# HGRN's 32-token attention blocks on column groups and diagonal tiles, and dt's contraction tiles accumulated in place

## The chip, the cores and the metric

The kernel runs on one core of a Trainium2 chip. The metric is the device time of one execution in microseconds; shown are the median and the spread of three timed runs. Beside them there is a profile of one execution, taken by the hardware profiler, with the start and the duration of each instruction on each engine: TensorE (PE; its weight loads are listed as PEld), VectorE (DVE), ScalarE (ACT), GpSimd (POOL) and SyncE's DMA queue (SPq).

## The reference, cut to what matters

Two transformer blocks run one after the other on 256 tokens of width 1024, all in float32. The first mixes with an SSD and an RWKV branch; its input projection also makes `dt`, eight columns, one for each SSD head. The second mixes with an HGRN2 branch (4 heads of width 128) and an attention branch (MoBA), and goes on with cross-attention and an MLP. The parts that the change touches:

```
dt = softplus((xn @ w_in)[:, dt columns] + dt_bias)          # first block, 8 columns

# second block, HGRN2, C = 32 tokens a chunk, n = 8 chunks, 4 heads
b      = cumsum(log f) within a chunk
q_t    = q * exp(b);   k_t = k * exp(-b);   k_end = k * exp(b_last - b)
A      = where(causal, q_t k_t^T, 0)          # 32 x 32 for each chunk and head
o      = A v + q_t state                      # inside the chunk + from the chunks before
state  = decay * state + k_end^T v            # from chunk to chunk
o      = rms_norm(o) * gain * silu(gate)
```

## The kernel before

One program is written out by hand for each engine; the order on an engine is the order of the code, and engines wait for one another on semaphores (`mark` counts a step, `at` names the count to wait for). Nothing is scheduled by a planner. All 256 tokens stay in SBUF. Wide projections are split into two float16 halves by ScalarE and VectorE (lines 537 and 569) and multiplied in three float16 products (line 623); the small products of the mixers stay in float32. One float32 matmul stands in the trace as two records, each with its weight load.

**dt, first block.** Behind the tiles of the low-rank columns, TensorE makes dt's projection: eight contraction tiles `k` of 128 rows, each a matmul with 32 weight columns (the eight dt columns are the last of them) and 256 streamed tokens. Tile `k` goes to column group `k % 4` of the array (its output stands on PSUM partitions 32·(k % 4) and on) and to half `k // 4` of bank 5, so eight separate partial products lie there (line 958). VectorE scales them all by the norm's rate into `dt_parts`, 128x512 (line 1042). One tile of the r columns later, `pe_dt_fold` adds them up by two float32 matmuls with a selecting matrix (line 905), and ScalarE adds the bias (line 1127). The fold waits for the constants, which the POOL queue loads while w_in is still landing. Around it TensorE works on w_in's tiles (line 623).

**HGRN, second block.** `pe_project2` sets TensorE's order. The 256 tokens are cut into two groups `c` of 128, each with four 32-token chunks. `pe_hgrn` makes, for each `c` and head `j`, the product of all 128 keys with all 128 queries (`KF`, `HQ`; line 2739) into bank 4 + c, four heads side by side, 512 columns. `dve_hgrn` multiplies by the mask `chunk32` (line 2792), 128x128, which keeps the causal half of the four 32x32 blocks on the diagonal and sets all else to 0; the result is `AM[c]`. TensorE meanwhile turns `k_end` to token-major (line 2745) and works on a tile of the MoBA keys' projection (line 623), a small rotary product on four column groups (line 2859) and another tile of line 623. Then come the state products of single chunks (line 2756), the MoBA values (line 2540), and `pe_hgrn_out(c)`: `AM[c]` times the values `VI` into bank 6 + c (line 2767), and on top of it, for each chunk, the queries times the state before (line 2773), on column groups. VectorE carries the state from chunk to chunk (line 2805). Behind the HGRN stretch come the gate's projection, the MoBA attention, the turning of the output (line 2785) and the output projection (line 739), for which VectorE and ScalarE have to make halves first.

Small tiles stand elsewhere in the same kernel too. Line 1900, in RWKV's block solve of the first block, runs float32 matmuls with 32x32 weights and 16 streamed columns on the four diagonal tiles of the array, 16 for each of the two head groups, all of a group into one bank. Line 2000, RWKV's state update, has 64 weight columns on two column groups and streams 64. Line 1663 is the first TensorE work of RWKV's preparation, behind ScalarE's line 1708.

Of the kernel before, what the change touches and what calls it, by code (L numbers as in the profile page):

```python
# [17 lines left out]
ALU = mybir.AluOpType  # L18
# [5 lines left out]
P = 128  # L24
T = 256
D = 1024
KT = D // P
C = 128
# [25 lines left out]
W_SCALE = 64.0  # L54
# [17 lines left out]
for _name, _tiles in PARAM_TILES:  # L72
# [6 lines left out]
BASE = 32  # L79
# [2 lines left out]
    ("incl", P), ("strict", P), ("neg_incl", P),  # L82
    ("ident32", BASE), ("pair32", BASE), ("levels", BASE // 2 * len(LEVELS)),
    ("blocks64", 2 * BASE),
    ("chunk32", P), ("causal", T), ("swap", P), ("cos", T), ("sin", T),
    ("reset128", T), ("reset32", T),
]
CONST_AT = {}
# [7 lines left out]
def constant_table():  # L96

    out = np.zeros((P, CONST_COLS), np.float32)

    def put(name, value):  # L100
        at, w = CONST_AT[name]
        out[:value.shape[0], at:at + w] = value

    r, c = np.arange(P)[:, None], np.arange(P)[None, :]
    put("ident", np.eye(P))
    put("ones", np.ones((P, P)))
    put("head_ones", (r // RW_HD == c // RW_HD) * 1.0)
    put("incl", (r <= c) * 1.0)
    put("strict", (r < c) * 1.0)
    put("neg_incl", (r <= c) * -1.0)  # L110
    r32, c32 = r % BASE, np.arange(BASE)[None, :]
    put("ident32", (r32 == c32) * 1.0)
    put("pair32", ((c32 == r32 + 1) & (c32 % 2 == 1)) * -1.0)
    put("blocks64", (np.arange(2 * BASE)[None, :] // BASE == r // BASE % 2) * -1.0)
    levels = []
    for m in LEVELS:

        mask = ((r32 // (2 * m) == c32 // (2 * m)) & (r32 % (2 * m) >= m) & (c32 % (2 * m) < m)) * 1.0
        levels.append(mask.reshape(P, BASE // (2 * m), 2, m)[:, :, 0, :].reshape(P, BASE // 2))
    put("levels", np.concatenate(levels, axis=1))  # L120
    put("chunk32", ((r <= c) & (r // HG_CHUNK == c // HG_CHUNK)) * 1.0)
    q, k = np.arange(P)[:, None], np.arange(T)[None, :]
    put("causal", np.where(k - P <= q, 0.0, -3e38))
    half = ROT // 2
    swap = np.zeros((P, P))
    for i in range(half):
        swap[i + half, i] = 1.0
        swap[i, i + half] = 1.0
    put("swap", swap)
    inv = np.float32(ROPE_THETA) ** (-np.arange(half, dtype=np.float32) * np.float32(2.0) / np.float32(ROT))  # L130
    ang = np.arange(T, dtype=np.float32)[:, None] * inv[None, :].astype(np.float32)
    cos, sin = np.cos(ang).T, np.sin(ang).T
    put("cos", np.concatenate([cos, cos]))
    put("sin", np.concatenate([-sin, sin] * MB_HEADS))
    t = np.arange(T)[None, :].repeat(P, 0)
    put("reset128", (t % C != 0) * 1.0)
    put("reset32", (t % HG_CHUNK != 0) * 1.0)
    return out
# [170 lines left out]
def build(nc, w, out, known):  # L309

    with ExitStack() as ctx:
# [38 lines left out]
        def const(name):  # L350
            a, n = CONST_AT[name]
            return consts[:, a:a + n]
# [60 lines left out]
        zs = view(SOLVE + 4128, 4, T)  # L413
        BTOKS = view(SOLVE + 5152, 2, SSD_STATE)
        dtT, aT, dtmp = view(SOLVE + 7168, T), view(SOLVE + 5664, T), view(SOLVE + 5920, T)
        dt_parts = view(SOLVE + 5664, 2, T)
        dtok = view(SOLVE + 6176, NC_, 8)
        atok = view(SOLVE + 6192, NC_, 8)
        cstok = view(SOLVE + 6208, NC_, 8)
# [480 lines left out]
        def pe_dt_fold(pe):  # L900

            pe.wait_ge(*at("dt raw"))
            pe.wait_ge(*at("constants landed"))
            for i in range(2):
                mm = nc.tensor.matmul(banks[6][0:SSD_HEADS, 0:T], const("ident32")[:, BASE - SSD_HEADS:BASE],
                                      dt_parts[:, i, :], start=(i == 0), stop=(i == 1))
            mm.then_inc(*mark("proj1_dt", "dt folded"))

        def pe_project1(pe):
            pe_project1_first(pe)  # L910
            for i, (kind, j) in enumerate(TILE_OF):
# [42 lines left out]
                if kind == "lora" and j == 1:  # L954

                    for k in range(KT):
                        q = BASE * (k % 4)
                        mm = nc.tensor.matmul(halves(5)[q:q + BASE, k // 4, :], slot("w_in", "lora")[:, k, 232:264],
                                              hg[:, k, :], start=True, stop=True, tile_position=(0, q))
                    mm.then_inc(*mark("proj1_dt", "proj1 dt"))  # L960
                    chunk_used("w_in", "lora", 0, ("proj1 dt",))
                elif j == dict(PROJ)[kind] - 1:
                    if ("w_in", kind, 0) in SPLIT_NO:
                        split_used(("w_in", kind, 0), ("proj1", b))
                    else:
                        chunk_used("w_in", kind, 0, ("proj1", b))
# [64 lines left out]
        def dve_project1_rwkv(dve):  # L1031
            lora_low(dve)
            norm_reciprocal(dve, "pre_mix")
            dve.wait_ge(*so_far("norm_rstd"))
            for b in range(7):
                dve.wait_ge(*at("proj1", b))
                if b == 0:
                    dve.wait_ge(*at("pads"))
                evacuate1(raw[:, 2 * b:2 * b + 2, 1:T + 1], b).then_inc(*mark("proj1_scaled", "proj1 out", b))
                if b == 2:  # L1040
                    dve.wait_ge(*at("proj1 dt"))
                    nc.vector.scalar_tensor_tensor(dt_parts, halves(5), 1.0 / W_SCALE, over(rstd[:, :], 2), ALU.mult,
                                                   ALU.mult).then_inc(*mark("dt_raw", "dt raw"))
                if b in (0, 2):
                    split_low(dve, b // 2, range(4))
                if b == 3:
                    split_low(dve, 2, range(4))
                if b == 4:
                    dve_shift(dve, range(3))
                    bc_low(dve, (0, 1))  # L1050
                if b == 5:
                    bc_low(dve, (2,))
            bc_low(dve, (3,))
            dve_shift(dve, range(3, 7))
# [1460 lines left out]
        FR, BCS, EB, EMB, HQ, KF = (view(1024 * i, 4, T) for i in range(6))  # L2515
        KETOK, VI = view(1024, NC_, HG_D), view(7168, NC_, HG_D)
        GH = view(8192, 4, T)
        AM = [view(512 * i, 4, C) for i in range(2)]
        NS = T // HG_CHUNK
        SV = [view(a, 4 * C) for a in (3072, 3584, 5120, 5632, 13312, 15872)] + [ssum[:, :]]  # L2520
        ON = view(3072, NC_, HG_D)
# [210 lines left out]
        def pe_hgrn(pe):  # L2732
# [3 lines left out]
            pe.wait_ge(*at("k~"))  # L2736
            for c in range(NC_):
                for j in range(4):
                    mm = nc.tensor.matmul(quarters(4 + c)[:, j, :], KF[:, j, c * C:(c + 1) * C],
                                          HQ[:, j, c * C:(c + 1) * C], start=True, stop=True)  # L2740
                mm.then_inc(*mark("hgrn_pe", "A bank", c))
            pe.wait_ge(*at("k end"))
            for c in range(NC_):
# [18 lines left out]
        def pe_hgrn_out(pe, c):  # L2762
# [1 line left out]
            pe.wait_ge(*at("A", c))  # L2764
            pe.wait_ge(*at("k end token-major", c))
            for j in range(4):
                nc.tensor.matmul(quarters(6 + c)[:, j, :], AM[c][:, j, :], VI[:, c, j * C:(j + 1) * C],
                                 start=(j == 0), stop=False, skip_group_check=True)
            pe.wait_ge(*at("hgrn state", 4 * c + 2))
            for j in range(4):  # L2770
                for n in range(max(1, 4 * c), 4 * c + 4):
# [17 lines left out]
        def dve_hgrn(dve):  # L2789
            for c in range(NC_):  # L2790
                dve.wait_ge(*at("A bank", c))
                nc.vector.tensor_tensor(AM[c], quarters(4 + c), over(const("chunk32"), 4), ALU.mult).then_inc(
                    *mark("hgrn_vector", "A", c))

        def dve_hgrn_state(dve, n):
            dve.wait_ge(*at("hgrn state bank", n))
# [786 lines left out]
```

## Time and profile before

| | |
|---|---|
| timed runs | 742.17, 743.42 and 743.67 us; median 743.42 |
| the profiled execution | span 741.7 us from its first to its last instruction, the one time that its page gives |
| TensorE busy | 730.6 us, 98% |
| VectorE, ScalarE, GpSimd busy | 576.3, 435.5 and 47.1 us |
| chain that ended last | TensorE 78%, VectorE 12%, ScalarE 4%, DMA 4% |
| A products, line 2739 | 16 records in 1.79 us |
| A times V, line 2767 | 2 x 8 records, 0.89 us each |
| dt's fold, line 905 | 4 records |

The chain of work that ended last is followed back from the last instruction, at each step to what released it. A group in it holds the time from the end of what came before it to its own end. Time saved in a group that is not in the chain shortens nothing by itself. Matmuls are pipelined: the duration of one record covers its way through the array, so the rate of a group is read from the starts of groups or from the chain, not from the duration of one.

### The profile page before, as it was taken

The numbers are of one execution on the slowest core, as the hardware profiler recorded it, in microseconds if no ns is written. First come the engines' busy times: TensorE is split into PE (matmuls) and PEld (weight loads), VectorE is DVE, ScalarE is ACT, GpSimd is POOL, SyncE is SP. The second block draws the span as 40 slices with busy tenths as digits, with TensorE's granted clock in tenths as the row PEclk, the third lists the DMA queues.
The fourth block names the chain that finished last, engine by engine and source line by source line (L and its number), as shares of the span: only waits on it lengthen the run. The fifth ranks groups of instructions, "written<-read, shape, count | busy, mean of one in ns | idle before, by whom it ended". The sixth has DMA issues, their size and how long they took to land.

```text
span 741.7 us, 16496 instructions
## 1 busy us (share of the span) xinstructions
PE 730.6 (98%) x7072; PEld 597.3 (81%) x7072; DVE 576.3 (78%) x908; ACT 435.5 (59%) x679; POOL 47.1 (6%) x81
## 2 busy tenths in 40 slices
PE   9999999999999999999999999999999999999997
PEld 6888877889778888888877686898888888865553
DVE  5899976777889999998678887899786666762444
ACT  5699872523656766666656573487584655653342
POOL 0000133040020000000002000003003000000000
PEclk9999999999999999999999999999999999999999
DMA  9990303512574566557690743339326165566001
GB/s 316 395 401 5 114 17 139 206 38 81 179 275 146 196 228 224 177 175 253 240 353 1 266 189 114 115 114 340 116 89 252 48 241 174 221 227 219 37 0 58
DMA packets 67146, 129.43 MB, mean 174 GB/s; under 512 B 3969, under 2 KB 28033, under 8 KB 66817
## 3 DMA queue, kind: packets, MB, share of 16 engines
q1 hardware_dynamic: 66032, 126.07, 47.2%
q0 software_dynamic: 320, 1.61, 0.6%
q8 instruction: 56, 0.92, 0.5%
q10 hardware_dynamic: 720, 0.70, 0.3%
q14 instruction: 18, 0.14, 0.1%
HBM read 127.32 MB, written 1.05 MB: 173 GB/s over the span
## 4 chain that ended last, share of the span: by engine, by line
PE 78%; DVE 12%; ACT 4%; DMA 4%; issue 1%; SPq 0%; DVEq 0%; ACTq 0%
PE bank L623 35%; PE bank L3218 11%; PE bank L739 11%; DVE arena L569 3%; PE bank L2540 3%; DMA ring<-in_w_in_dram 2%; PE bank L1551 2%; PE bank L874 1%; PE bank L1570 1%; PE bank L1832 1%; DMA ring<-in_ffn_w_up_dram 1%; PE bank L893 1%; DVE arena L1076 1%; PE bank L1885 1%; PE bank L2012 1%
## 5 line engine op out<-in xcount | busy, mean ns | idle before, releaser
L623 PE MATMUL bank<-hg,arena 128*128 128x256 f16 x2496 | 275.4, 273 | 1.5 <-DVE arena L556 1.1
L623 PEld LDWEIGHTS bank<-hg,arena 128*128 128x128 f16 x2496 | 243.6, 98 | 32.6 <-issue 2.6
L569 DVE SCALAR_TENSOR_TENSOR arena<-ring,arena 128x1024 f16<-128x1024 f32 x150 | 175.5, 1227 | 52.7 <-ACT arena L537 52.7
L537 ACT ACTIVATE arena<-ring 128x1024 f16<-128x1024 f32 x150 | 146.6, 1044 | 83.8 <-PE bank L3218 37.6
L3218 PE MATMUL bank<-arena 128*128 128x512 f16 (+1 forms) x480 | 83.6, 336 | 0.0
L3218 PEld LDWEIGHTS bank<-arena 128*128 128x128 f16 x480 | 47.0, 98 | 36.1
L739 PE MATMUL bank<-arena 128*128 128x256 f16 x528 | 57.8, 273 | 0.0
L739 PEld LDWEIGHTS bank<-arena 128*128 128x128 f16 x528 | 51.7, 98 | 6.0
L556 DVE SCALAR_TENSOR_TENSOR arena<-ring,arena 128x2048 f16<-128x2048 f32 x22 | 50.4, 2292 | 0.7
L739 PE MATMUL bank<-mix,arena 128*128 128x256 f16 x384 | 42.2, 273 | 0.0
L549 ACT ACTIVATE arena<-ring 128x2048 f16<-128x2048 f32 x22 | 41.7, 1895 | 0.0
L739 PEld LDWEIGHTS bank<-mix,arena 128*128 128x128 f16 x384 | 37.6, 98 | 4.3
L2491 ACT ACTIVATE arena<-arena,params 128x256 f32<-128x256 f32 x44 | 20.0, 500 | 31.8 <-DVE arena L2437 31.8
L623 PE MATMUL bank<-xv,arena 128*128 128x256 f16 x336 | 37.4, 273 | 0.2 <-issue 0.2
L2448 DVE SCALAR_TENSOR_TENSOR arena<-arena,params 128x256 f32<-128x256 f32 x88 | 36.7, 479 | 0.7 <-ACT arena L2491 0.7
L623 PEld LDWEIGHTS bank<-xv,arena 128*128 128x128 f16 x336 | 32.5, 98 | 5.4 <-DVE arena L569 0.8
L638 ACT ACTIVATE hg<-h,params 128x256 f16<-128x256 f32 x32 | 15.9, 498 | 26.4 <-DVE h L799 13.4
L658 POOL TENSOR_TENSOR ssum<-sqs 128x256 f32<-128x256 f32 x4 | 2.9, 728 | 351.8 <-ACT sqs L642 351.8
L3172 DVE SCALAR_TENSOR_TENSOR arena<-bank,rstd 128x512 f32<-128x512 f32 x16 | 11.0, 690 | 16.3 <-PE bank L623 16.3
L648 DVE SCALAR_TENSOR_TENSOR hg<-h,params,hg 128x256 f16<-128x256 f32 x32 | 20.4, 658 | 3.9 <-ACT hg L638 3.9
L1570 PE MATMUL bank<-arena,xk 128*128 128x512 f16 x96 | 21.4, 379 | 0.0
L2540 PE MATMUL bank<-arena,hg 128*128 128x512 f16 x96 | 21.2, 379 | 0.0
(425 smaller groups left out, 992.5 us busy)
## 6 DMA issues: line engine op xcount, KB each, us to landing
ring<-in_w_in_dram SPq DMA_DIRECT2D x12, 2048.0 KB, 9.7
ring<-in_ffn_w_up_dram SPq DMA_DIRECT2D x22, 1024.0 KB, 7.8
ring<-in_w_ff_dram SPq DMA_DIRECT2D x8, 2048.0 KB, 8.9
ring<-in_w_ff_dram SPq DMA_DIRECT2D x16, 1024.0 KB, 6.6
ring<-in_ffn_w_down_dram SPq DMA_DIRECT2D x11, 1024.0 KB, 6.6
ring<-in_w_out_dram SPq DMA_DIRECT2D x8, 1024.0 KB, 7.7
ring<-in_w_xk_dram SPq DMA_DIRECT2D x2, 2048.0 KB, 11.8
ring<-in_w_xv_dram SPq DMA_DIRECT2D x2, 2048.0 KB, 10.3
```

Source lines behind the costliest of these rows:

```text
L537: nc.scalar.activation(quarter(halves_of(chunk)[0], chunk, q), quarter(slot(*chunk), chunk, q), ACT.Copy, scale=W_SCALE).then_inc(*mark("w ...
L549: nc.scalar.activation(pair_of(halves_of(chunk)[0], chunk, q), pair_of(slot(*chunk), chunk, q), ACT.Copy, scale=W_SCALE).then_inc(*mark("w ...
L556: nc.vector.scalar_tensor_tensor(pair_of(halves_of(chunk)[1], chunk, q), pair_of(slot(*chunk), chunk, q), W_SCALE, pair_of(halves_of(chunk ...
L569: nc.vector.scalar_tensor_tensor(quarter(halves_of(chunk)[1], chunk, q), quarter(slot(*chunk), chunk, q), W_SCALE, quarter(halves_of(chunk ...
L623: mm = nc.tensor.matmul(out_, weight[a][:, k, cols], src[:, k, b, :], start=(first and i == 0), stop=(last and i == 2), skip_group_check=True)
L648: nc.vector.scalar_tensor_tensor(hg16[:, m, 1, :], h[:, m, :], par(gain, m), hg16[:, m, 0, :], ALU.mult, ALU.subtract).then_inc(*mark("nor ...
L739: mm = nc.tensor.matmul(out_, weight, moving[:, k, b, :], start=(first and n == 0), stop=(last and n == 2), skip_group_check=True)
L1570: mm = nc.tensor.matmul(banks[2 + c][:, :], mem16[:, k, x, c * C:(c + 1) * C], w_[a][:, k, :], start=(k == 0 and i == 0), stop=(k == KT - ...
L2448: nc.vector.scalar_tensor_tensor(uacc[r][:, i, :], uraw[r][:, i, tap:tap + T], par("ffn_conv_w", 2 * FFT * tap + tile0 + i), uacc[r][:, i, :],
L2491: nc.scalar.activation(uacc[r][:, i, :], uraw[r][:, i, 2:T + 2], ACT.Copy, scale=par("ffn_conv_w", 2 * 2 * FFT + 2 * p + FFT * (b % 2) + i ...
L2540: mm = nc.tensor.matmul(banks[bank][:, :], hg16[:, k, b, c * C:(c + 1) * C], w_[a][:, k, :], start=(k == 0 and n == 0), stop=(k == KT - 1 ...
L3218: mm = nc.tensor.matmul(last_bank(c, half, cols)[:, cols], hid2[:, k, x, c * C:(c + 1) * C], weight[a][:, k % 4, 512 * half + cols.start:5 ...
```

## The change

A products: instead of one 128x128 product for each head and token group, four products of 32 keys with 32 queries, one for each chunk. Chunk `b` goes to column group `b` and stands on PSUM partitions 32·b to 32·b + 31, head `j` in columns 32·j and on, so that a token group's blocks fill 128 columns of a bank instead of 512. The mask shrinks to 32 columns, the same causal triangle on each 32 partitions, and `AM[c]` to 128x128. A times V uses the block of chunk `b` as a 32x32 weight on the diagonal tile (row group `b`, column group `b`), against that chunk's 32 rows of values, 128 columns wide: 16 matmuls for 4. The matmuls of dt keep their number and their column groups, but tiles `k` and `k + 4` now accumulate in the same 256 columns, so VectorE scales 128x256 and the fold is one matmul. The table of constants loses 96 columns, and its load goes from 1056 KB to 1008 KB.

```
@@ constants
-    ("chunk32", P), ("causal", T), ("swap", P), ("cos", T), ("sin", T),
+    ("chunk32", BASE), ("causal", T), ("swap", P), ("cos", T), ("sin", T),
...
-    put("chunk32", ((r <= c) & (r // HG_CHUNK == c // HG_CHUNK)) * 1.0)
+    put("chunk32", (r % HG_CHUNK <= np.arange(HG_CHUNK)[None, :]) * 1.0)
@@ dt
-            for i in range(2):
-                mm = nc.tensor.matmul(banks[6][0:SSD_HEADS, 0:T], const("ident32")[:, BASE - SSD_HEADS:BASE],
-                                      dt_parts[:, i, :], start=(i == 0), stop=(i == 1))
-            mm.then_inc(*mark("proj1_dt", "dt folded"))
+            nc.tensor.matmul(banks[6][0:SSD_HEADS, 0:T], const("ident32")[:, BASE - SSD_HEADS:BASE], dt_parts,
+                             start=True, stop=True).then_inc(*mark("proj1_dt", "dt folded"))
...
-                        mm = nc.tensor.matmul(halves(5)[q:q + BASE, k // 4, :], slot("w_in", "lora")[:, k, 232:264],
-                                              hg[:, k, :], start=True, stop=True, tile_position=(0, q))
+                        mm = nc.tensor.matmul(banks[5][q:q + BASE, 0:T], slot("w_in", "lora")[:, k, 232:264],
+                                              hg[:, k, :], start=(k < 4), stop=(k >= 4), tile_position=(0, q),
+                                              skip_group_check=True)
...
-                    nc.vector.scalar_tensor_tensor(dt_parts, halves(5), 1.0 / W_SCALE, over(rstd[:, :], 2), ALU.mult,
+                    nc.vector.scalar_tensor_tensor(dt_parts, banks[5][:, 0:T], 1.0 / W_SCALE, rstd[:, :], ALU.mult,
@@ HGRN
-                    mm = nc.tensor.matmul(quarters(4 + c)[:, j, :], KF[:, j, c * C:(c + 1) * C],
-                                          HQ[:, j, c * C:(c + 1) * C], start=True, stop=True)
+                    for b in range(4):
+                        r, t = HG_CHUNK * b, c * C + HG_CHUNK * b
+                        mm = nc.tensor.matmul(banks[4 + c][r:r + HG_CHUNK, HG_CHUNK * j:HG_CHUNK * (j + 1)],
+                                              KF[:, j, t:t + HG_CHUNK], HQ[:, j, t:t + HG_CHUNK], start=True,
+                                              stop=True, tile_position=(0, r))
...
-                nc.tensor.matmul(quarters(6 + c)[:, j, :], AM[c][:, j, :], VI[:, c, j * C:(j + 1) * C],
-                                 start=(j == 0), stop=False, skip_group_check=True)
+                for b in range(4):
+                    q = slice(HG_CHUNK * b, HG_CHUNK * b + HG_CHUNK)
+                    nc.tensor.matmul(quarters(6 + c)[q, j, :], AM[c][q, j, :], VI[q, c, j * C:(j + 1) * C],
+                                     start=(j == 0), stop=False, tile_position=(HG_CHUNK * b, HG_CHUNK * b),
+                                     skip_group_check=True)
...
-                nc.vector.tensor_tensor(AM[c], quarters(4 + c), over(const("chunk32"), 4), ALU.mult).then_inc(
-                    *mark("hgrn_vector", "A", c))
+                nc.vector.tensor_tensor(AM[c], banks[4 + c][:, 0:P].rearrange("p (j n) -> p j n", j=4),
+                                        over(const("chunk32"), 4), ALU.mult).then_inc(*mark("hgrn_vector", "A", c))
```

No instruction changes its place on its engine. Here is what stands on TensorE in a row around the A products, before (the first row is the column form of the norm's rate, line 623 is a projection, 2745 turns k_end, 2859 is the rotary product; the shape is the output's, and a float32 matmul is one row here and two records in the trace):

```order
L697 MATMUL bank<-consts,rstd 128x1 x2
L623 MATMUL bank<-hg,arena 128x256 x144
L2739 MATMUL bank<-arena 128x128 x8
L2745 MATMUL bank<-consts,arena 128x128 x8
L623 MATMUL bank<-hg,arena 128x256 x24
L2859 MATMUL bank<-arena,consts 32x256 x4
```

And in the changed kernel, whose line numbers have moved a little:

```order
L697 MATMUL bank<-consts,rstd 128x1 x2
L623 MATMUL bank<-hg,arena 128x256 x144
L2740 MATMUL bank<-arena 32x32 x32
L2747 MATMUL bank<-consts,arena 128x128 x8
L623 MATMUL bank<-hg,arena 128x256 x24
L2864 MATMUL bank<-arena,consts 32x256 x4
```

Eight full products have become 32 small ones in the same place, between two groups on the full array. On TensorE around A times V of the first token group, before (2756 are state products, 2540 the MoBA values, 2773 queries times states, 2889 and 2890 MoBA scores):

```order
L2756 MATMUL bank<-arena 128x128 x8
L2540 MATMUL bank<-arena,hg 128x512 x24
L2767 MATMUL bank<-arena 128x128 x4
L2773 MATMUL bank<-arena 32x128 x12
L2756 MATMUL bank<-arena 128x128 x8
L2889 MATMUL bank<-arena 128x128
L2890 MATMUL bank<-arena 128x256
```

And now:

```order
L2758 MATMUL bank<-arena 128x128 x8
L2539 MATMUL bank<-arena,hg 128x512 x24
L2771 MATMUL bank<-arena 32x128 x16
L2778 MATMUL bank<-arena 32x128 x12
L2758 MATMUL bank<-arena 128x128 x8
L2894 MATMUL bank<-arena 128x128
L2895 MATMUL bank<-arena 128x256
```

Four full matmuls have become 16 on 32x32 tiles; the second token group changes in the same way.

## Rows read from the trace of the kernel before

**Rows 1.** The page: busy us (share) xinstructions of each engine; the chain's shares by engine.

```profile
PE 730.6 (98%) x7072; PEld 597.3 (81%) x7072; DVE 576.3 (78%) x908; ACT 435.5 (59%) x679; POOL 47.1 (6%) x81
...
PE 78%; DVE 12%; ACT 4%; DMA 4%; issue 1%; SPq 0%; DVEq 0%; ACTq 0%
```

**Rows 2.** The chain of work that ended last, HGRN stretch: start us, us, what.

```profile
443.59 1.79 PE bank L2739 x16
...
446.25 2.62 PE bank L623 x24
...
449.43 2.73 PE bank L623 x24
...
465.48 0.89 PE bank L2767 x8
...
475.36 0.89 PE bank L2767 x8
476.25 1.01 PE bank L2773 x32
```

**Rows 3.** The timeline, 436 to 470 us: start us, us, engine line op out<-in xcount [idle before].

```profile
443.43 1.95 PE L2739 MATMUL bank<-arena 128*128 128x128 f32 x16
...
445.38 1.28 DVE L2792 TENSOR_TENSOR arena<-bank,consts 128x512 f32<-128x512 f32 x2
...
449.50 0.43 DVE L2874 TENSOR_TENSOR bank<-bank,consts 128x256 f32<-128x256 f32 x1 [2.84 <-PE bank L2859]
```

**Rows 4.** The timeline of TensorE, 119 to 127 us.

```profile
120.10 0.73 PE L1900 MATMUL bank<-arena 32*32 32x16 f32 x64
120.76 1.48 PE L1551 MATMUL bank<-xk,sqs 128*128 128x256 f16 x12
```

**Rows 5.** The timeline of TensorE, 137 to 140 us.

```profile
137.71 1.15 PE L2000 MATMUL bank<-arena 128*64 128x64 f32 x32
138.69 1.48 PE L2012 MATMUL bank<-arena 128*64 128x128 f32 x24
```

**Rows 6.** The chain of work that ended last, first 68 us.

```profile
18.60 18.16 DMA ring<-in_w_in_dram
...
66.33 0.95 ACT arena L1708
...
67.33 0.76 PE bank L1663 x5
```

**Rows 7.** Who waited for whom, VectorE and ScalarE, 426 to 512 us: us, times, longest.

```profile
DVE arena L2805 <- PE bank L2756: 3.6, 2, 2.0
...
ACT mix L2965 <- PE bank L2912: 1.4, 2, 0.7
```

**Rows 8.** Who waited for whom, TensorE, whole span: us, times, longest.

```profile
PE bank L1663 <- ACT arena L1708: 0.6, 1, 0.6
```

**Rows 9.** The timeline, 27.9 to 36.2 us.

```profile
28.16 0.68 DVE L1042 SCALAR_TENSOR_TENSOR arena<-bank,rstd 128x512 f32<-128x512 f32 x1
...
31.39 4.63 DVE L569 SCALAR_TENSOR_TENSOR arena<-ring,arena 128x1024 f16<-128x1024 f32 x4 [2.55 <-ACT arena L537]
...
33.08 1.03 PE L905 MATMUL bank<-arena,consts 128*8 128x256 f32 x4
...
34.04 2.36 PE L623 MATMUL bank<-xv,arena 128*128 128x256 f16 x20
```

**Rows 10.** DMA issues, 10 to 60 us (KB, us to landing); then a stretch, DMA share, GB/s.

```profile
consts<-in_constants_dram POOLq DMA_DIRECT2D x1, 1056.0 KB, 9.1
...
22.00:26.00 4.00, 4.00 (x45) 2.93 (x44) 3.79 (x5) 4.00 (x6) 1.36 (x3) 1.00 1.05 404
```

**Rows 11.** Stretches: us, busy us (xcount) by engine, granted clock, DMA share, GB/s.

```profile
110.00:115.00 5.00, 5.00 (x58) 3.73 (x55) 0.63 (x3) 0.26 (x1) 0.00 (x0) 0.85 0.01 3
115.00:120.00 5.00, 5.00 (x113) 3.89 (x112) 3.90 (x11) 1.65 (x2) 0.00 (x0) 0.80 0.02 3
...
440.00:446.00 6.00, 6.00 (x57) 5.65 (x56) 6.00 (x8) 2.49 (x4) 0.00 (x0) 1.00 0.31 128
```

More of the change, by code:

```diff
@@ L415, in build @@
         dtT, aT, dtmp = view(SOLVE + 7168, T), view(SOLVE + 5664, T), view(SOLVE + 5920, T)
-        dt_parts = view(SOLVE + 5664, 2, T)
+        dt_parts = view(SOLVE + 5664, T)
         dtok = view(SOLVE + 6176, NC_, 8)
@@ L2517, in build @@
         GH = view(8192, 4, T)
-        AM = [view(512 * i, 4, C) for i in range(2)]
+        AM = [view(512 * i, 4, HG_CHUNK) for i in range(2)]
         NS = T // HG_CHUNK
```

## The prediction

> **What bounds the kernel now.** I read the page's busy times first, then the chain of work that ended last, then the two stretches that the change touches. TensorE is busy 98% of the span and holds 78% of that chain [rows 1], so a microsecond of TensorE counts only where the chain runs through TensorE. In the HGRN stretch it does: from 443 to 490 us the chain goes from one TensorE group straight to the next, and the three groups that the change rewrites stand in it by name [rows 2]: the A products (line 2739) and the two A times V products (line 2767). In the dt stretch it does not: from 18.60 to 36.76 us the chain is the landing of w_in, after that VectorE and ScalarE, and TensorE comes back only at 67.33 us, where it had waited 0.6 us for ScalarE's line 1708 [rows 6, 8].
>
> **The A products.** Before, 8 matmuls of 128x128 make 16 records (one f32 matmul is two) [rows 3], and they hold 1.79 us of the chain [rows 2], 0.112 us a record. Three quarters of what they make is masked away. After, 32 matmuls of 32x32 make 64 records, four of them side by side on the four column groups, each streaming 32 columns instead of 128. The nearest rows are those of line 1900: 64 f32 records, also four side by side, 32 columns loaded and 16 streamed, start at 120.10 us, and the next group starts at 120.76: 0.66 us, with the way out into a full-array group in it [rows 4]. The way in costs something too. 24 matmuls of line 623 behind another full-array group hold 2.62 us, the same 24 behind the 32-row rotary matmuls 2.73 [rows 2]: a change of tile shape costs 0.11. So the new A costs 0.66 + 0.11 = 0.77 us, and the term is 0.77 - 1.79 = **-1.02 us**. The trace has no f32 tile of 128 rows by 32 columns that streams as few columns as it loads. The row that bounds it on the dear side is line 2000, which loads 64 columns of 128 rows and streams 64: 32 records in sixteen pairs from 137.71 to 138.69 us, 0.98 us [rows 5]. If a round of four new tiles took as long as such a pair, A would cost 0.98 + 0.11 = 1.09, a gain of 0.70. I take 1.02, since line 1900 has the same number of records, rounds and loaded columns; what it lacks is 96 rows of weights and 16 streamed columns. Nothing in the rows is quicker than line 1900, so the gain's upper end is 1.1.
>
> **A times V.** Before, 4 matmuls (8 records) for each of the two 128-token chunks hold 0.89 us [rows 2]. After, 16 matmuls (32 records) on four diagonal 32x32 tiles, each still streaming 128 columns. Four side by side therefore last as long as one full matmul: the stream isn't shortened, only rows and columns of the array are left out. The row like it is line 2773 of the second chunk: 32 f32 records, four side by side, 128 streamed columns, 1.01 us with its own change of shape [rows 2]. So each product goes from 0.89 to 1.01, **+0.12**, twice: **+0.24 us**. The change of shape behind it (into line 2773) was there before. This is what the smaller A tile costs, for the compact block can only be used on diagonal tiles.
>
> **VectorE's masking.** Two products of 128x512 take 1.28 us and become 128x128. Behind them VectorE waits 2.84 us for TensorE's rotary matmul [rows 3], so this is worth nothing here. It only uncovers a longer wait; the cover would have to shrink by 2.84 us before it counted.
>
> **Does the HGRN gain reach the end?** Later work on VectorE and ScalarE in this stretch waits for TensorE and not the other way: VectorE's state update waits 3.6 us in all for line 2756, ScalarE's copies of the MoBA output 1.4 us for line 2912 [rows 7]. These waits move with TensorE; where a stage's release is not moved at all, 0.7 us (the longest wait of line 2965) of the 0.78 would still pass. I count the whole: -1.02 + 0.24 = **-0.78 us**.
>
> **dt.** The eight dt matmuls stay eight and of the same shape; only their start and stop flags and half of their addresses change: 0. VectorE's scaling of 128x512 (0.68 us) becomes 128x256, which saves at most half, 0.34; but the next VectorE group waits 2.55 us for ScalarE, which waits for w_in to land [rows 9]: 0. The fold's four records run from 33.08 to 34.04 us, 0.96 [rows 9]; two of them fall away, some 0.43 us of TensorE. TensorE then reaches the wait at 67.33 us that much sooner and waits 1.0 instead of 0.6 [rows 8]: 0. It would be worth 0.43 if the chain ran through TensorE there.
>
> **The constants.** The mask shrinks from 128 to 32 columns, so the load of 1056 KB becomes 1008 KB. It runs in the very stretch in which the chain is the landing of w_in, at 404 GB/s over all engines [rows 6, 10]. 48 KB at that rate is **-0.12 us**, at least 0 if the two don't share engines evenly.
>
> **Sum.** -0.78 - 0.12 = -0.90 us. The profiled execution has a span of 741.7 us, 1.7 below the median of 743.42; nothing in the change touches what lies around the span. 743.42 - 0.90 = **742.5 us**. With the bounds (A's gain 0.70 to 1.1, the constants 0 to 0.12, the fold 0 to 0.43) the sum lies between -0.46 and -1.41, 742.0 to 743.0, and the timed runs themselves spread from 742.17 to 743.67.
>
> **Rivals.** *Small records start one by one.* If the records, not the rounds of four, set the pace, with line 2000's 0.98 / 32 = 31 ns a record, 64 of them take 1.96 + 0.11 = 2.07 us, and A loses 0.28; the sum is 0.28 + 0.24 - 0.12 = +0.40, 743.8. Against it: line 1900's 64 records in 0.66 us are 10 ns each [rows 4]. The Trainium skill states such a floor ("TensorE: Matmul & The Clock Gate", section "Wait — 56ns, not 53.3ns?"): starts never closer than about 25 ns however few columns are streamed. By that rule A would take 1.6 + 0.11 = 1.71 us, the sum would be +0.04, and the trace's 10 ns contradict it for tiles that lie side by side. Chance 0.07.
>
> *Diagonal tiles that write one bank take turns: slower.* All four diagonal tiles of A times V write one PSUM bank from different rows of the array. If they ran one after the other, each of the 32 records would cost what a full record does, 0.89 / 8 = 0.111 us: 3.56 + 0.11 = 3.67 for 0.89, +2.78 twice; the sum is -1.02 + 5.56 - 0.12 = +4.4, 747.8. It turns the sign as soon as the two products together lose over 1.14 us. Against it: line 1900 also runs four diagonal tiles into one bank, and at 10 ns a record they overlap. But it streams only 16 columns, so a conflict would show less there. The Trainium skill says of row tiles that they can't use the same PSUM bank at the same time ("TensorEngine Tiling (Array Packing)", section "Gotcha 1: PSUM Pressure"); line 1900's 0.66 us [rows 4] speak against it. Chance 0.03.
>
> *The gain is taken back before 490 us*, by a VectorE or ScalarE chain that doesn't move with TensorE: only the constants are left, 743.3. Chance 0.07; rows 7 speak against it.
>
> *The clock.* The granted clock is 1.00 in every stretch around the change, but between 110 and 120 us it is 0.85 and then 0.80 [rows 11], behind small matmuls: lost clock of 0.75 + 1.00 = 1.75 us at most. A similar fall to 1.2 GHz at the new small matmuls would give 742.5 + 1.75 = 744.3 at most (0.04), and the fall at 110 us gone, through a shift of the work, 740.8 at least (0.04).
>
> *The fold counts*: 742.1 (0.05). *A at its dear bound*: 742.8 (0.08).
>
> **How the numbers follow.** That leaves 0.62 for the forecast. A measurement of this kernel can tell about 0.2%, 1.5 us, from no change; the forecast is 0.9 below, so it would mostly read as the same. Given the spread of the runs I let a quarter of its 0.62 fall below 741.9, half of the fold's case and all of the lifted clock: 0.22 faster. Slower holds the turn-taking tiles and a little of the clock's fall: 0.04. The rest, 0.74, is the same. The range takes the bounds of the sum, the first and third rivals and most of the spread of the runs: 741.4 to 743.9.
>
> **What would show it.** In the changed kernel the chain's A group should hold 64 records in some 0.7 to 0.8 us where 1.79 stood, with four starts close together and then a short pause; each A times V group 32 records in 1.0 us; VectorE's two masks some 0.6 us together and the wait behind them longer; the fold two records; the wait before line 1663 longer than 0.6 us; w_in's landing at 36.76 some 0.1 us earlier. It is wrong if the A records stand 20 ns or more apart, if the A times V group goes over 1.5 us, if TensorE waits between 445 and 490 us where it didn't, or if the clock falls in that stretch.

## The result and the profile after

The changed kernel takes 744.99 us (median of 20 runs, 743.15 to 747.44) and the kernel before, beside it, 743.64 (20 runs, 742.17 to 744.48). The ratio is 1.0024, with a 95% interval of 1.0015 to 1.0032: slower by some 1.8 us, where 0.9 us less was forecast. (The ratio is not the quotient of the two medians, which lie 1.35 us apart; prices in us are taken from the ratios, here and below, unless the text says otherwise.) The profiled execution has a span of 742.6 us (741.7 before) and an own time of 744.4.

The page of the changed kernel (busy us, share of the span, instructions; then the shares of the chain of work that ended last), to be held against [rows 1]:

```profile
PE 729.5 (98%) x7166; PEld 595.6 (80%) x7166; DVE 575.4 (77%) x908; ACT 435.4 (59%) x679; POOL 47.0 (6%) x81
...
PE 78%; DVE 12%; ACT 5%; DMA 4%; issue 1%; SPq 0%; DVEq 0%; ACTq 0%
```

TensorE has 1.1 us less work and 94 records more (96 more in A and A times V, two less in the fold), and yet the span is longer. The sum of the busy times doesn't say where it went; the chain does. The chain of the changed kernel (start us, us, what; it counts 50 of A's 64 records, the timeline further down has them all):

```profile
26.05 17.24 DMA ring<-in_w_in_dram
...
194.33 9.16 DMA ring<-in_ffn_w_up_dram
...
445.08 0.69 PE bank L2740 x50
445.77 1.02 PE bank L2747 x8
...
466.02 1.01 PE bank L2771 x32
...
476.02 1.01 PE bank L2771 x32
...
490.84 0.60 ACT mix L2970
```

The HGRN groups behave as forecast against [rows 2]: A holds 0.69 us where 1.79 stood, each A times V product 1.01 where 0.89 stood. But the A products begin at 445.08 us and not at 443.59. The loss lies ahead of them, where nothing of HGRN has run yet: the landing of w_up, for one, holds 9.16 us of the chain. The same rows of the kernel before, with the end of its HGRN stretch:

```profile
193.50 8.50 DMA ring<-in_ffn_w_up_dram
...
490.07 0.60 ACT mix L2965
```

I then laid VectorE's instructions of the two traces beside each other, in the order of the program, and took the difference of their starts. The changed kernel is late by 1.5 us at 49 us, by 0.5 at 116 and 0.3 at 120, by 0.8 at 159, by 1.5 again at 206 and by 0.8 at 484. The step at 116 to 120 us belongs to TensorE's clock. The kernel before was granted 0.85 and 0.80 from 110 to 120 us in its profiled execution [rows 11]; the changed kernel, in the same two stretches (us, busy us and count by engine, granted clock, DMA share, GB/s):

```profile
110.00:115.00 5.00, 4.58 (x64) 4.42 (x65) 1.85 (x8) 1.32 (x3) 0.51 (x2) 1.00 0.01 3
115.00:120.00 5.00, 5.00 (x116) 3.64 (x114) 3.42 (x9) 1.65 (x2) 0.00 (x0) 1.00 0.01 3
```

So the two spans alone, 0.9 us apart, hide 1.2 us: that execution of the kernel before had lost it to the clock, this one had not. What is left is lateness of 1.5 us that arises before 50 us and of 0.7 around 204 us, in the two stretches in which the chain is the landing of weights, and half a microsecond at 155 us, among RWKV's small matmuls, where the DMA engines are all but idle. From 22 to 40 us (the same columns), first the kernel before, then the changed one:

```profile
22.00:40.00 18.00, 18.00 (x167) 14.72 (x166) 13.99 (x15) 13.09 (x19) 1.36 (x3) 1.00 1.05 395
```

```profile
22.00:40.00 18.00, 18.00 (x170) 14.92 (x167) 13.37 (x15) 12.63 (x18) 1.76 (x3) 1.00 1.04 378
```

The DMA engines are as busy (a share of 1.05 and 1.04) and move 378 GB/s where they moved 395. The forecast had no term for that. The change's one touch on any DMA is the table of constants, 96 columns of fp32 shorter.

### The profile page after: what moved, and what is told of

The parts are those of the page before. It is cut to its first block, busy times and chain, and to the rows that moved or that the text cites. A ratio compares the mean times of both kernels' runs of the same rounds, so it can differ in the third digit from the quotient of the medians.

```text
span 742.6 us, 16684 instructions
## 1 busy us (share of the span) xinstructions
PE 729.5 (98%) x7166; PEld 595.6 (80%) x7166; DVE 575.4 (77%) x908; ACT 435.4 (59%) x679; POOL 47.0 (6%) x81
## 3 DMA queue, kind: packets, MB, share of 16 engines
HBM read 127.27 MB, written 1.05 MB: 173 GB/s over the span
## 4 chain that ended last, share of the span: by engine, by line
PE 78%; DVE 12%; ACT 5%; DMA 4%; issue 1%; SPq 0%; DVEq 0%; ACTq 0%
PE bank L623 35%; PE bank L3223 11%; PE bank L739 11%; PE bank L2539 3%; DVE arena L569 3%; DMA ring<-in_w_in_dram 2%; PE bank L1550 2%; PE bank L874 1%; PE bank L1569 1%; DMA ring<-in_ffn_w_up_dram 1%; PE bank L1831 1%; PE bank L893 1%; PE bank L2011 1%; DVE arena L611 1%; PE bank L819 1%
```

## Experiments

Each edit is timed in five rounds against the kernel before on the same chip. The first four ran together, the next four, the next three, and the last one alone.

**Which part of the change it is.** Two causes were open: the landings, through the table, and the clock, through the new small matmuls, in executions that no profile shows. Three kernels carry one part each, and the fourth is the whole change again. HGRN alone has the change's hunks in HGRN, with the table of constants left as wide as before (its mask uses the first 32 of 128 columns):

```
-    put("chunk32", ((r <= c) & (r // HG_CHUNK == c // HG_CHUNK)) * 1.0)
+    put("chunk32", (r % HG_CHUNK <= np.arange(P)[None, :]) * 1.0)
...
+  ... over(const("chunk32")[:, 0:HG_CHUNK], 4), ALU.mult)
```

> The kernel before with the HGRN edits alone (A on column groups, A times V on diagonal tiles, the smaller mask product); the table of constants keeps its size, so the SBUF layout and the transfers are those of before; dt as before. Theory clock: the small tiles leave TensorE so little to do between 445 and 480 us that its clock is lowered to 1.2 GHz there in many executions; then this kernel has mean granted clocks down to 0.993 to 0.997 in its timed runs, a wide spread, and a median 0.5 to 2 us above before although the profile's HGRN groups are 0.78 us shorter. Theory layout: the loss comes from the smaller table of constants and the 384 bytes by which all of SBUF moves; then this kernel is 0.6 to 0.8 us faster than before, with the clocks of before.

Measured: 742.06 us against 743.32, ratio 0.9988 (0.9977 to 0.9999). The HGRN edits gain some 0.9 us, near the 0.78 of the sum. Its executions had mean granted clocks of 0.993 to 1.000, those of the kernel before that they are compared with 0.996 to 1.000, and it was the quicker one all the same: the small matmuls don't cost it the clock in its median.

dt alone has only the change's hunks in dt.

> The kernel before with the dt edits alone (accumulated in one half bank, scaled 128x256, one fold matmul). Theory clock and theory layout both: within 0.3 us of before, since the fold is off the chain. A third theory, that the shorter fold lets TensorE run into the stage behind it in another way: 0.5 us or more off, in either direction.

Measured: 743.55 against 743.32, ratio 1.0000 (0.9991 to 1.0009). No gain is seen, as forecast; but the interval is 0.7 us to either side, and the fold's 0.43 us could hide in it.

The table alone is the kernel before, with another table cut by the same 96 columns. The rotary swap table is used in its first 32 columns only, so no instruction changes but the load:

```
-    ("chunk32", P), ("causal", T), ("swap", P), ("cos", T), ("sin", T),
+    ("chunk32", P), ("causal", T), ("swap", BASE), ("cos", T), ("sin", T),
...
-    put("swap", swap)
+    put("swap", swap[:, 0:BASE])
```

> The kernel before with another table cut from 128 to 32 columns (the rotary swap matrix, of which only 32 columns are used), so that the load of constants and the place of everything in SBUF behind it are exactly those of the changed kernel, and the program is that of before. Theory layout: 1 to 2 us slower than before, the packets of w_in between 20 and 40 us some 5% longer (90 ns against 86) and w_in's landing that ends the first chain 1 us later. Theory clock: as before, or 0.1 us faster.

Measured: 745.41 against 743.32, ratio 1.0025 (1.0015 to 1.0035). A kernel that loads 48 KB less and does nothing else differently is slower by some 1.9 us. The window of 22 to 40 us in its trace:

```profile
22.00:40.00 18.00, 18.00 (x168) 14.72 (x166) 13.75 (x15) 12.44 (x17) 1.76 (x3) 1.00 1.04 379
```

and in the trace of HGRN alone:

```profile
22.00:40.00 18.00, 18.00 (x168) 14.72 (x166) 14.49 (x16) 13.59 (x19) 1.62 (x3) 1.00 1.05 397
```

379 GB/s with the shorter table, 397 with the table as it was: the slow landings come and go with the table, and neither with HGRN nor with dt.

> The changed kernel once more beside the kernel before on this chip. Both theories: 1.0 to 1.8 us slower than before. Theory clock: the slow executions are those with a low mean clock. If instead the difference came from the chip of the first comparison, it is 0.5 to 1 us faster here.

Measured: 743.91 against 743.32, ratio 1.0010 (1.0001 to 1.0019); 379 GB/s in the window. The whole change is again slower than before, by 0.7 us, which is less than in the first comparison and less than both theories expected; the two intervals overlap from 1.0015 to 1.0019 only. The parts add up to -0.12 + 0.00 + 0.25 = +0.13%.

**What about a shorter table makes landings slower.** The constants are the first tensor in SBUF, and params and the weight ring follow. Cutting 96 columns moves all that lies behind by 384 bytes in each partition. The ring, into which every weight lands, began at byte 11392 of a partition, counted from the start of the constants by the widths in the code, 128 over a multiple of 256; now it begins at 11008, a multiple of 256. If the address counts and not the load, unused columns ahead of the ring must give the time back, and take it away from the kernel before. Four kernels put them there:

```
         consts = sb("consts", CONST_COLS)
+        sb("pad", 96)
         params = sb("params", PARAM_COLS)
         ring = sb("ring", RING, SLOT)
```

The changed kernel with 96 columns has its ring at 11392 again.

> The changed kernel with an unused 96-column tile in SBUF behind the table of constants, so that all of SBUF behind it stands where it stood before, while the table and its load stay small (1008 KB). Theory address (the place of the weight ring in SBUF sets how fast the weights land): as the HGRN edits alone, 0.8 to 1.4 us faster than before, packets of w_in at 84 ns. Theory transfer (the smaller load, or what it moves in HBM, is what costs): 0.6 to 1.5 us slower than before, packets at 88 ns.

Measured: 741.95 against 742.86, ratio 0.9988 (0.9978 to 0.9999). 384 unused bytes in each partition turn the change from slower to faster.

The kernel before with 32 columns there has its ring at 11520, a multiple of 256, and its load of constants untouched.

> The kernel before with an unused 32-column tile behind the table of constants: its table and load stay at 1056 KB, but the ring and all behind it move up by 128 bytes, to the same remainder of 512 bytes (256) as in the changed kernel. Theory address: 1.5 to 2.5 us slower than before, packets of w_in at 87 to 88 ns. Theory transfer: as before, 84 ns.

Measured: 745.61 against 742.86, ratio 1.0031 (1.0016 to 1.0045): the loss without any part of the change.

The changed kernel with 64 columns (11264, a multiple of 512) asks whether a rounder address is better.

> The changed kernel with an unused 64-column tile there: the ring begins at a multiple of 512 bytes. Theory address: not the time of the changed kernel; if whole multiples suit the packets best, 1.0 to 2.5 us faster than before; if 128 bytes over a multiple was a lucky place, 0 to 2 us slower. Theory transfer: as the changed kernel, 0.6 to 1.5 us slower than before.

Measured: 744.58 against 742.86, ratio 1.0016 (1.0002 to 1.0029): it isn't.

The changed kernel with 32 columns (11136, again 128 over a multiple of 256, but not the place of the kernel before) asks whether it is that one place or the remainder.

> The changed kernel with an unused 32-column tile there: the ring begins 384 bytes over a multiple of 512. Theory address: packets differ from one of the other places; 128 and 384 may be alike (84 ns, 0.8 to 1.4 us faster than before) if it is the multiple of 256 that costs. Theory transfer: as the changed kernel.

Measured: 742.19 against 742.86, ratio 0.9987 (0.9977 to 0.9997): it is the remainder. The window of 22 to 40 us in the four traces, with 96 columns in the changed kernel, 32 in the kernel before, 64 and 32 in the changed kernel:

```profile
22.00:40.00 18.00, 18.00 (x170) 14.92 (x168) 14.19 (x15) 13.56 (x19) 1.70 (x3) 1.00 1.05 396
```

```profile
22.00:40.00 18.00, 18.00 (x167) 14.72 (x166) 13.02 (x14) 12.38 (x17) 1.76 (x3) 1.00 1.05 377
```

```profile
22.00:40.00 18.00, 18.00 (x169) 14.93 (x168) 13.12 (x15) 12.36 (x17) 1.76 (x3) 1.00 1.04 377
```

```profile
22.00:40.00 18.00, 18.00 (x170) 14.92 (x168) 14.05 (x15) 13.41 (x19) 1.54 (x3) 1.00 1.05 397
```

396 and 397 where the ring begins 128 over, 377 and 377 on a multiple of 256. The pair of the changed kernel with and without 96 columns is the cleanest, since both run the same instructions. The chain with the 96 columns (its lines are one further down):

```profile
25.68 15.95 DMA ring<-in_w_in_dram
...
192.10 8.56 DMA ring<-in_ffn_w_up_dram
...
442.26 0.69 PE bank L2741 x50
442.95 1.02 PE bank L2748 x8
...
463.20 1.00 PE bank L2772 x32
...
473.20 1.00 PE bank L2772 x32
...
488.02 0.60 ACT mix L2971
```

The landing of w_in holds 15.95 us where 17.24 stood, that of w_up 8.56 where 9.16 stood. VectorE without the columns is late by 0.9 us at 23 us, 1.6 at 49, 2.0 at 154 and 2.8 at 203, behind w_up, and stays so to the end (742.6 against 739.7 us of span). Not all of that is landings: 0.6 us of it arises between 150 and 159 us, where the chain without the columns has TensorE pause twice for 0.14 us inside line 1899 (0.55 + 0.14 + 0.37 us for a group that holds 0.72 with the columns) and no weight is waited for. The traces of the whole change again and of the 64 columns below, compared with the same one, are later by 0.3 us and by nothing there, so at least half of that step belongs to this one execution. Without it the spans give the price of the landings as 2.9 - 0.6 = 2.3 us, and the ratios of two such kernels timed together (1.0016 with 64 columns, 0.9988 with 96) as 0.28%, 2.1 us.

The DMA issues between 20 and 60 us (KB, us from issue to landing), without and with the 96 columns, show the load that was to bring the gain:

```profile
ring<-in_w_xk_dram SPq DMA_DIRECT2D x1, 2048.0 KB, 15.6
...
consts<-in_constants_dram POOLq DMA_DIRECT2D x1, 1008.0 KB, 9.2
```

```profile
ring<-in_w_xk_dram SPq DMA_DIRECT2D x1, 2048.0 KB, 14.7
consts<-in_constants_dram POOLq DMA_DIRECT2D x1, 1008.0 KB, 8.8
```

The smaller load itself took 9.2 us, not less than the 9.1 of before [rows 10], and 8.8 with the ring back in its place; that it was held up by the weights, which land more slowly on the same engines, is likely but not shown.

**The ring, or what lies behind it.** Columns ahead of the ring move everything behind it too. Two kernels separate them: the changed kernel with 32 columns ahead and 32 more behind the ring (ring 128 over; all behind it at the changed kernel's remainder), and one with 32 behind the ring alone (the other way round). Params, ahead of the ring, moves with it.

```
+        sb("pad", 32)
         params = sb("params", PARAM_COLS)
         ring = sb("ring", RING, SLOT)
+        sb("pad_behind", 32)
```

> The changed kernel with 32 unused columns ahead of the weight ring and 32 behind it: the ring begins 128 bytes over a multiple of 256, all that stands behind it (activations, arena) a whole multiple of 256, as in the changed kernel. Theory ring (only the place that the DMA writes counts): as the changed kernel with its padding, 0.8 to 1.4 us faster than before, packets at 84 ns. Theory rest (what the engines read and write while the weights land, the arena and the activations, is what must stand at 128): 0.6 to 1.5 us slower than before, packets at 88 ns.

Measured: 742.19 against 743.49, ratio 0.9988 (0.9979 to 0.9997).

> The changed kernel with 32 unused columns behind the weight ring alone: the ring stays at a whole multiple of 256 bytes, all behind it moves to 128 over one. Theory ring: as the changed kernel, 0.6 to 1.9 us slower than before, packets at 88 ns. Theory rest: 0.8 to 1.4 us faster than before, 84 ns.

Measured: 745.46 against 743.49, ratio 1.0025 (1.0013 to 1.0037). The place of the ring, with params that move with it, is all of it; what lies behind the ring doesn't count. The windows of the two:

```profile
22.00:40.00 18.00, 18.00 (x169) 14.92 (x168) 14.01 (x16) 13.13 (x18) 1.76 (x3) 1.00 1.04 393
```

```profile
22.00:40.00 18.00, 18.00 (x170) 14.93 (x168) 12.81 (x14) 11.45 (x16) 1.76 (x3) 1.00 1.05 377
```

**Other remainders.** With 16 columns the ring begins at 11072, 64 over a multiple of 256, and with 48 at 11200, 192 over.

> The changed kernel with 16 unused columns behind the table of constants: the ring begins 64 bytes over a multiple of 256. If only whole multiples of 256 are slow: packets at 84 ns and 0.8 to 1.4 us faster than before. If 128 is the one good place: packets above 84 ns and slower than before.

Measured: 745.51 against 743.49, ratio 1.0026 (1.0016 to 1.0037).

> The changed kernel with 48 unused columns behind the table of constants: the ring begins 192 bytes over a multiple of 256. If 128 over is the one good place among multiples of 64: packets slower than 84 ns, 0.6 to 2.2 us slower than before. If 192 is good too: 84 ns and 0.8 to 1.4 us faster than before.

Measured: 745.85 against 742.55, ratio 1.0040 (1.0026 to 1.0053): 3.0 us slower, more than the 2.2 that was expected at most. The windows of the two:

```profile
22.00:40.00 18.00, 18.00 (x170) 14.93 (x168) 12.85 (x15) 12.34 (x17) 1.76 (x3) 1.00 1.04 375
```

```profile
22.00:40.00 18.00, 18.00 (x169) 14.91 (x168) 13.19 (x15) 12.50 (x18) 1.76 (x3) 1.00 1.04 378
```

Of the four remainders, in steps of 64 bytes, 128 alone is good:

| ring begins, bytes over a multiple of 256 | kernels | GB/s, 22 to 40 us | packet of 2048 bytes, median, 40 to 55 us |
|---|---|---|---|
| 128 | before, HGRN alone, dt alone, 96 columns, 32 columns, ring alone | 393 to 397 | 84 ns |
| 0 | changed, table alone, before with 32, 64 columns, rest alone | 377 to 379 | 88 ns |
| 64 | 16 columns | 375 | 88 ns |
| 192 | 48 columns | 378 | 88 ns |

Finer steps than 64 bytes weren't tried, nor another tensor than the ring.

## Why the prediction was wrong, step by step

**The constants: the step that failed.** The prediction gave the shorter table -0.12 us, "at least 0 if the two don't share engines evenly". It priced the table as bytes of one load. Cut alone, the table costs +0.25%, 1.9 us (1.1 to 2.6 by the interval of its ratio), through a route that was not in the list: it is the first tensor in SBUF, so its width sets the address of the weight ring, and 384 bytes put every weight landing in a place where the same DMA engines, as busy as before, move 4 to 5% less (22 to 40 us). The bound "at least 0" had no row behind it; the diff alone tells that everything behind the table moves. The landing that was to end 0.1 us earlier than 36.76 us [rows 6] ends later. The changed kernel's chain takes another piece of w_in, but that of the table alone has one that begins 0.7 us later than the row of before:

```profile
19.26 18.82 DMA ring<-in_w_in_dram
```

It ends at 38.08 us, 1.3 us later, and took 18.82 us for 18.16.

**A products: right.** Forecast 0.66 + 0.11 us for 1.79. The timeline of the changed kernel (start us, us, engine line op, tile, shapes, records):

```profile
445.01 0.76 PE L2740 MATMUL bank<-arena 128*32 128x32 f32 x64
...
445.70 1.09 PE L2747 MATMUL bank<-consts,arena 128*128 128x128 f32 x8
...
446.87 0.48 DVE L2797 TENSOR_TENSOR arena<-bank,consts 128x128 f32<-128x128 f32 x2
...
450.05 0.43 DVE L2879 TENSOR_TENSOR bank<-bank,consts 128x256 f32<-128x256 f32 x1 [2.70 <-PE bank L2864]
```

From the first A record to the first transpose 0.69 us pass. The transposes behind now hold 1.02 us of the chain where they held 0.87 in the kernel before:

```profile
445.38 0.87 PE bank L2745 x8
```

The change of tile shape now lies there, and the two groups together go from 1.79 + 0.87 = 2.66 to 0.69 + 1.02 = 1.71: -0.95 for a forecast of -1.02. Line 1900 was the right row to price it by: 128 rows and 32 streamed columns cost no more than its 32 and 16.

**A times V: right.** 1.01 us for 0.89, twice, +0.24. The rows of the first product and of the group behind it:

```profile
465.95 1.08 PE L2771 MATMUL bank<-arena 32*32 32x128 f32 x32
...
466.96 1.07 PE L2778 MATMUL bank<-arena 128*32 128x128 f32 x24
```

32 records in 1.01 us on four diagonal tiles that write one bank: they run side by side.

**VectorE's masks: right.** 0.48 us for 1.28 [rows 3], worth nothing: VectorE waits 2.70 us behind them, 2.84 before. The wait was to grow and did not: the masks end 0.80 us sooner, but TensorE's products, and with them the rotary matmul, come 0.95 us sooner.

**Does the HGRN gain reach the end: right.** From the start of A to line 2965 (now 2970) 490.07 - 443.59 = 46.48 us pass before and 490.84 - 445.08 = 45.76 after, a gain of 0.72; the terms measured give -0.95 + 0.24 = -0.71. Alone, the HGRN edits gain 0.12% (0.01 to 0.23) at the end, and the three versions of the change with the ring 128 over a multiple of 256 gain as much.

**dt: right in its sizes; what it is worth is not settled.** VectorE's scaling takes 0.41 us for 0.68, the fold two records from 33.89 to 34.42 us, 0.53 for 0.96 [rows 9]. The changed kernel's timeline:

```profile
29.40 0.41 DVE L1041 SCALAR_TENSOR_TENSOR arena<-bank,rstd 128x256 f32<-128x256 f32 x1
...
33.89 0.60 PE L904 MATMUL bank<-arena,consts 128*8 128x256 f32 x2
34.42 3.34 PE L623 MATMUL bank<-xv,arena 128*128 128x256 f16 x29
```

The wait ahead of line 1663 (now 1662) was to go from 0.6 to 1.0 us. It is 1.7:

```profile
PE bank L1662 <- ACT arena L1707: 1.7, 1, 1.7
```

but the late weights are in this number: with the ring back in its place the same wait is 0.4 us, so the forecast of 1.0 is not borne out. The wait that was to swallow dt's gain isn't a fixed reserve either. In the traces of HGRN alone and of dt alone it is not there at all: from 25 to 67 us their chain is TensorE's own work, and the fold stands in it, first as before, then as one matmul:

```profile
33.41 0.96 PE bank L905 x4
```

```profile
34.10 0.53 PE bank L904 x2
```

So, with the ring 128 over a multiple of 256, TensorE and the landings end this stretch within a microsecond of each other, and which of them ends last differs from one trace to the next. The forecast's 0 for the fold came from one execution in which the landings did. The time of dt alone doesn't tell 0 from 0.43 us.

**The rivals.** Small records one by one fell: 0.69 us for 64 records is 10.8 ns each, the way in with it, and not 31. The rule of the Trainium skill that was weighed there ("TensorE: Matmul & The Clock Gate", section "Wait — 56ns, not 53.3ns?"), starts never closer than about 25 ns, doesn't hold for these tiles side by side: in the trace the first starts come in fours 7 ns apart, a four every 32 ns. Diagonal tiles that take turns fell at 1.01 us against 3.67; the skill's rule on one PSUM bank ("TensorEngine Tiling (Array Packing)", section "Gotcha 1: PSUM Pressure") doesn't show in these products. The gain taken back before 490 us fell with the 45.76 us, A at its dear bound with the 0.69 us; the fold is open, as said. The fall of the clock at the new matmuls would have given about the time that came, 744.3, but by another cause. In the changed kernel's HGRN stretch it stays at full speed (2.4 GHz):

```profile
440.00:491.00 51.00, 50.99 (x559) 38.83 (x557) 42.33 (x98) 24.14 (x43) 0.00 (x0) 1.00 0.30 110
```

The clock does move single executions: of HGRN alone, five at a mean clock below 0.998 took 742.9 to 745.0 us, and seven at 0.998 or over 741.1 to 742.2. But both kernels have such executions, and the ring's price stands at an equal clock too: of the executions at 0.999 or over, those of the kernel before with 32 columns took 744.1 to 745.4 us, those of the kernel before beside it 742.0 to 743.5, and those of the changed kernel with 96 columns 741.1 to 742.3. The other half of that rival, the fall at 110 us gone, is what the two profiled executions show, and in them it covered part of the loss. The HGRN and dt edits don't take it away: the changed kernel with 32 columns has the fall (0.74 and 0.92), while HGRN alone lacks it (1.00 in both stretches). What decides it is open. None of the rivals was the one that came: a loss through the landings had no case, and the range ended at 743.9.

## What to carry to other kernels

A table or tile that changes its size moves all that is laid out behind it, so compute the new start of whatever the DMAs write and the DMA rate of the weight-bound stretches before a term is given to the edit itself; unused columns can hold the old place (96 here) or a place as good (32). Here a weight ring 128 bytes over a multiple of 256 was worth some twice the whole gain in HGRN or more, and a version that beats both kernels, by little, is the change with 96 unused columns ahead of the ring: 741.95 us, 0.9988 (0.9978 to 0.9999) of the kernel before. A path that ends just behind the longest one, as TensorE's does ahead of line 1663, can be the longest in the next execution, so a wait of 0.6 us in one profile is no proof that a gain there is worth nothing. And where two profiles of nearly the same time are compared, lay their instructions beside each other in program order and look for the steps: a difference of 0.8 us at the end was 1.5 late by 49 us, 1.2 regained by 120, 1.2 lost again by 206 and 0.7 regained in HGRN.

## What the runs showed of the hardware

- The rate of a landing depends on its address in SBUF. With the ring 128 bytes over a multiple of 256, packets of 2048 bytes took 84 ns at the 10%, 50% and 90% marks (20 to 40 us, the changed kernel with 96 columns); without the columns 84, 87 and 95 ns, and packets of 1024 bytes (232 to 330 us) 55 ns at the 90% mark for 46. That only a part of the packets is slower is what the traces show; what makes them so is open.
- The Trainium skill says in "DMA: Bandwidth & Descriptors", section "How a descriptor splits into AXI transactions", that a descriptor which starts at a multiple of 256 bytes splits into transactions of 256 bytes and a leftover, and that with another start the first transaction begins at the boundary below, and what it fetches ahead of the start is unused but still costs beats of the transfer. Taken for the destinations here, it would be the other way round from what was measured: multiples of 256 gave 377 to 379 GB/s, 128 over 393 to 397, and 64 and 192 over no better than a multiple. The section speaks of what is fetched and not of the side that is written; for that side the measurement decides.
- Full fp32 tiles of 128 rows by 32 columns on the four column groups cost no more a record than 32 by 32 ones: 64 records streaming 32 columns in 0.69 us, against 0.66 for line 1900's [rows 4].
